# Half of the tail's gate products made inside the sample attention, with a ring of five slots

## The reference

```python
u = rmsnorm(x, g_mix)
proj = jnp.einsum('btd,df->btf', u, w_in)
(q_nsa, kv_nsa, g_nsa, qkv_gdn, b_gdn, a_gdn, z_gdn, q_mem, g_br) = jnp.split(proj, ...)
o_nsa, o_gdn, o_mem = ...            # sparse attention, gated delta rule, attention into memory tokens
gates = jax.nn.sigmoid(g_br.astype(jnp.float32)).reshape(B, T, N_BRANCH, D_MODEL)
merged = (gates[:, :, 0] * jnp.einsum('btc,cd->btd', o_nsa, w_br_nsa)
          + gates[:, :, 1] * jnp.einsum('btc,cd->btd', o_gdn, w_br_gdn)
          + gates[:, :, 2] * jnp.einsum('btc,cd->btd', o_mem, w_br_mem))
h = x + jnp.einsum('btd,de->bte', merged, w_out)
y = h + relu(rmsnorm(h) @ w_ff1)^2 @ w_ff2
```

## Time and profile before

| | |
|---|---|
| median of 3 runs | 1644.3 us (1639.56 to 1644.61) |
| the profiled execution | 1641.88 us, span 1640.1 us |
| mean granted clock | 0.925 |
| PE busy | 1461.0 us (89%) |
| PE weight loads | 1342.2 us (82%) |
| DVE busy | 871.5 us (53%) |
| ACT busy | 383.5 us (23%) |
| DMA | 159 MB, mean 97 GB/s |

### The profile page before, as it was taken

How to read it: one execution, slowest core, us unless ns; L and a number is a source line. 1 busy time by engine, 2 the same in 40 slices (tenths; PEclk the granted TensorE clock), 3 DMA queues, 4 the chain that set the end, 5 groups by cost and what they waited for, 6 DMA issues and landing times. The chain is left out here.

```text
span 1640.1 us, 27038 instructions
## 1 busy us (share of the span) xinstructions
PE 1461.0 (89%) x11343; PEld 1342.2 (82%) x11343; DVE 871.5 (53%) x1590; ACT 383.5 (23%) x891; POOL 82.5 (5%) x76
## 2 busy tenths in 40 slices
PE   6999899889968797989766689999989999999998
PEld 5778789789958586868543389899988999999998
DVE  3555256848633556564433355545746746465563
ACT  3543023222232344454221231000003101000000
POOL 1000001100011111111100000000000000000000
PEclk8999999999967697979678789999999999999999
DMA  9232035151321000010258442333240332323321
GB/s 351 72 116 97 13 95 184 56 201 57 119 53 53 0 1 1 2 52 2 100 190 312 175 124 79 107 99 95 91 156 26 104 104 78 103 80 99 93 88 53
DMA packets 115649, 159.03 MB, mean 97 GB/s; under 512 B 6040, under 2 KB 106840, under 8 KB 112779
## 3 DMA queue, kind: packets, MB, share of 16 engines
q1 hardware_dynamic: 111886, 122.76, 23.4%
q0 software_dynamic: 2304, 33.56, 5.1%
q10 hardware_dynamic: 1348, 1.12, 0.2%
HBM read 145.04 MB, written 16.66 MB: 99 GB/s over the span
## 5 line engine op out<-in xcount | busy, mean ns | idle before, releaser
L330 PE MATMUL ps<-uH,wh 128*128 128x260 f32 x576 | 165.9, 288 | 8.7 <-DVE wt L301 8.7
L330 PE MATMUL ps<-hH,wh 128*128 128x260 f32 x512 | 144.9, 283 | 2.6 <-DVE hT L301 2.6
L330 PE MATMUL ps<-mergedH,wh 128*128 128x260 f32 x512 | 145.7, 285 | 0.0
L330 PE MATMUL ps<-mergedT,wh 128*128 128x260 f32 x512 | 144.8, 283 | 0.0
L330 PE MATMUL ps<-hT,wh 128*128 128x260 f32 x512 | 144.8, 283 | 0.0
L330 PE MATMUL ps<-mergedH,wl 128*128 128x260 f32 x512 | 144.5, 282 | 0.0
L330 PE MATMUL ps<-hH,wl 128*128 128x260 f32 x512 | 144.5, 282 | 0.0
L457 PE MATMUL ps<-XT,w 128*128 128x256 f32 (+1 forms) x512 | 125.5, 386 | 6.3 <-DVE XT L520 6.0
L330 PEld LDWEIGHTS ps<-uH,wh 128*128 128x128 f32 x576 | 109.9, 191 | 13.6 <-DVE wt L301 8.9
L330 PE MATMUL ps<-uL,wh 128*128 128x260 f32 x384 | 109.1, 284 | 0.0
L330 PE MATMUL ps<-uH,tw 128*128 128x260 f32 x384 | 109.0, 284 | 0.0
(11 more groups left out here) (525 smaller groups left out, 3470.8 us busy)
## 6 DMA issues: line engine op xcount, KB each, us to landing
wt<-in_w_ff SPq DMA_DIRECT2D x32, 1024.0 KB, 5.4
wt<-in_w_in SPq DMA_DIRECT2D x15, 1024.0 KB, 5.7
tw<-in_w_in SPq DMA_DIRECT2D x12, 1024.0 KB, 5.3
ring<-in_cache_mem_kv SPq DMA_DIRECT2D x4, 2048.0 KB, 11.2
w<-in_cmp_w SPq DMA_DIRECT2D x8, 512.0 KB, 7.7
ring<-in_cache_win_kv SPq DMA_DIRECT2D x2, 2048.0 KB, 9.8
out_s_win<-in_cache_win_kv SPq DMA_DIRECT2D x1, 4088.0 KB
scratch_uhigh<-uH SPq DMA_DIRECT2D x1, 2080.0 KB
```

The lines of the kernel that those rows point to most:

```text
L330: ins = pe.matmul(out, lhsT(i, c), rhs(j, c), start=(first and c == 0 and k == 0), stop=(last and c == chunks - 1 and k == 2))
```

## The change

1. The gate products of tokens 0 to 255 (`TOKA`) move into the sample attention. A gate tile is made there in two halves of 512 rows, 24 halves in all (`GS`), numbered g. A half is loaded by SP (512 KB, three buffers `gr`), its high part made by ACT (two buffers `gh`), its low part by DVE, and PE makes 24 matmuls of 256 columns into bank 4. After two halves ACT copies the bank to `staged` and SP writes it to memory (256 KB). The steps' places are `gate_keys`.
2. The tail makes gates for tokens 256 to 519 only (264 tokens, two units for each tile in place of four), from the same full weight tiles. It loads the stored sums (`sums`), and ACT takes their sigmoid in one instruction.
3. Weight tiles' high parts are made by ACT in the tail (`highs`); DVE makes the low parts alone.
4. The ring has five slots in place of seven. SP no longer waits for the piece before.
5. `u` of the first 256 tokens is loaded at the stage's start; `u` of the others into the same place after the last half.
6. The scores of the new token are made in the compressed step, kept in `newk`, and read from there.

```diff
-        self.filled = [self.sem(f"e_slot{k}") for k in range(7)]
+        self.filled = [self.sem(f"e_slot{k}") for k in range(5)]
...
+        gate_keys = [0.4, 0.45, 0.7, 5.6, 5.7, 15.5, 19.0, 19.2, 19.4, 25.5, 29.0, 29.2, 29.4, 30.45, 30.7, 35.6, 35.7, 45.5, 49.0, 49.2,
+                     55.5, 55.6, 59.0, 59.2]
+        split_key = lambda g: gate_keys[g - 1] + 0.02 if g else 0.3
...
+            def gate_pe(pe):
+                for g in range(GS):
+                    q, half = g // 2, g % 2
+                    yield gate_keys[g]
+                    pe.wait_ge(g_split, g + 1)
+                    if g == 0:
+                        pe.wait_ge(u_in, 32)
+                    if half == 0 and q:
+                        pe.wait_ge(g_kept, q)
+                    w = g_wh[g % 2], g_low[g % 3]
+                    for m in range(WM):
+                        ins = self.product3(pe, ps[:, 4, TOKA * m:TOKA * (m + 1)], lambda i, c: w[i][:, c, m * P:(m + 1) * P],
+                                            lambda i, c: uA[i][:, HC * half + c, :], HC, first=half == 0 and m == 0, last=half == 1 and m == WM - 1)
+                    ins.then_inc(g_acc, 1)
...
+                def gates():
+                    yield -1.0
+                    for x, dram in zip(uA, self.u_dram):
+                        sp.dma_start(x.bitcast(F32)[:, :, :], dram[:, :, 0:TOKA]).then_inc(u_in, 16)
+                    for g in range(GS):
+                        yield -0.9 if g < 3 else gate_keys[g - 3] + 0.03
+                        if g >= 3:
+                            sp.wait_ge(g_acc, g - 2)
+                        rows = slice(HC * P * (g % 2), HC * P * (g % 2 + 1))
+                        sp.dma_start(g_raw[g % 3][:, :, :], gate_srcs[g // 2][rows, :].rearrange("(c p) n -> p c n", p=P)).then_inc(g_in[g % 3], 16)
+                    yield gate_keys[GS - 1] + 0.03
+                    sp.wait_ge(g_acc, GS)
+                    for x, dram in zip(self.uB, self.u_dram):
+                        sp.dma_start(x.bitcast(F32)[:, :, :], dram[:, :, TOKA:NT]).then_inc(self.u_back, 16)
...
+            def gate_high(act):
+                for g in range(GS):
+                    yield split_key(g)
+                    act.wait_ge(g_in[g % 3], 16 * (g // 3 + 1))
+                    if g >= 2:
+                        act.wait_ge(g_acc, g - 1)
+                    act.copy(g_wh[g % 2][:, :, :], g_raw[g % 3][:, :, :]).then_inc(g_high, 1)
+
+            def gate_sums(act):
+                for q in range(GS // 2):
+                    yield gate_keys[2 * q + 1] + 0.03
+                    act.wait_ge(g_acc, 2 * q + 2)
+                    if q >= 2:
+                        act.wait_ge(g_out[q % 2], 16 * (q // 2))
+                    act.copy(staged[q % 2], ps[:, 4, :].rearrange("p (a n) -> p a n", n=P)).then_inc(g_kept, 1)
...
+            def gate_low(dve):
+                for g in range(GS):
+                    yield split_key(g) + 0.005
+                    dve.wait_ge(g_high, g + 1)
+                    dve.tensor_tensor(g_low[g % 3][:, :, :], g_raw[g % 3][:, :, :], g_wh[g % 2].bitcast(F32)[:, :, :], ALU.subtract).then_inc(g_split, 1)
...
-        return [(m, slice(HALF * h, HALF * h + HALF)) for m in range(WM) for h in range(2)]
+        return [(m, tok) for m in range(WM) for tok in (slice(0, TOKA), slice(TOKA, NT))]
...
+                def sums():
+                    for q in range(Q):
+                        yield start[index["gate", q]] + 0.15 if q >= 2 else 0.05
+                        if q >= 2:
+                            sp.wait_ge(taken, NU * (q - 2) + 3)
+                        sp.dma_start(sig[:, q % 2, :, 0:TOKA], self.gate_dram[q].rearrange("p (m t) -> p m t", m=WM)).then_inc(sums_in[q % 2], 16)
...
+                            yield start[n] + 0.3
+                            act.wait_ge(sums_in[q % 2], 16 * (q // 2 + 1))
+                            act.activation(sig[:, q % 2, :, 0:TOKA], sig[:, q % 2, :, 0:TOKA], ACT.Sigmoid).then_inc(gatedA, 1)
+                            for m in range(WM):
+                                yield unit_at(n, m + 1)
+                                act.wait_ge(acc, acc_of("gate", q, m))
+                                if q >= 2:
+                                    act.wait_ge(taken, NU * (q - 2) + 2 * m + 2)
+                                act.activation(sig[:, q % 2, m, B], ps[:, (WM * q + m) % 2, 0:TOKB], ACT.Sigmoid).then_inc(gated, 1)
+
+                def highs():
+                    for n in range(NT_ + 1):
+                        yield start[n - 1] + 0.18 if n else 0.08
+                        k = k0 + n
+                        act.wait_ge(self.w_loaded[k % 2], self.loaded_at[k])
+                        if n >= 2:
+                            act.wait_ge(acc, self.tile_end[k - 2])
+                        cut = lambda x: x[:, 0:tiles[n][1], :]
+                        act.copy(cut(self.wh[k % 2]), cut(raw[n % 3])).then_inc(self.w_high, 1)
...
-                by_key(dense(), turn(), sample())
+                by_key(highs(), dense(), turn(), sample())
```

More of the change, by code:

```diff
@@ L1849, in stage_sample_attention @@
         ring = self.ring
+        at = self.taken["w1"][1]
+        for name in ("uH", "uL"):
+            self.taken[name] = (at, at + KC * TOKB)
+            at += KC * TOKB
         for k in range(len(ring), RING):
@@ L1969, in cmp_pe @@
                     ins = pe.matmul(rows32(0, j)[:, 0:NCMP], self.qblk[:, 4 * r + j, :], self.kcT[:, 4 * r + j, 0:NCMP], start=True, stop=True)
+                for j in range(4):
+                    for i in range(2):
+                        ins = pe.matmul(rows32(0, j)[:, P + i:P + i + 1], self.qblk[:, 4 * r + j, :], self.knT[:, i, 4 * r + j:4 * r + j + 1], start=True, stop=True)
                 ins.then_inc(c_s[r], 1)
@@ L2094, in load_free, with free_key @@
                         eng.wait_ge(v_done, n + 1)
+            def free_key(k):
+                if k < RING:
+                    return -0.8
+                n = job_of[k - RING]
+                if pieces[k - RING][0] == "memk":
+                    return turn_key(n, GROUPS["mem"] - 1, 3) + 0.05
+                return value_key(n, NPROB(jobs[n][0]) - 1) + 0.05
             @block.gpsimd
@@ L2104, in _ @@
             def _(sp):
[L2105 to L2121, removed]
+                def plain():
+                    for k, (what, r) in enumerate(pieces):
+                        if what == "sel":
+                            continue
+                        yield free_key(k)
+                        load_free(sp, k)
+                        if what == "win":
+                            src = I["cache_win_kv"][4 * r:4 * r + 4].rearrange("b (t p) v g d -> p (b t) (v g d)", p=P)
+                        else:
+                            src = I["cache_mem_kv"][4 * r:4 * r + 4, :, 0 if what == "memk" else 1].rearrange("b (t p) h d -> p (b t) (h d)", p=P)
+                        sp.dma_start(slot(k).rearrange("p (a c) -> p a c", a=src.shape[1]), src).then_inc(fetched[k % RING], 16)
+                    sel_last = max(n for n, (br, _) in enumerate(jobs) if br == "sel")
+                    yield value_key(sel_last, NPROB("sel") - 1) + 0.06
+                    sp.wait_ge(v_done, sel_last + 1)
+                    sp.dma_start(self.tw0[:, :, :], gate_srcs[0].rearrange("(c p) n -> p c n", p=P)).then_inc(self.w_loaded[self.issued % 2], 16)
@@ L2353, in stage_tail @@
         START = 5.0
[L2354 to L2357, removed]
+        start, ends = [START], [0]
+        units_of = lambda n: WM if seq[n][0] == "gate" else NU
+        for n, (kind, _) in enumerate(seq):
+            start.append(start[-1] + units_of(n) * (2.93 if kind == "gate" else 1.44))
+            ends.append(ends[-1] + units_of(n))
+        unit_at = lambda n, i: start[n] + i * (start[n + 1] - start[n]) / units_of(n)
         for n in range(NT_):
-            self.tile_end.append(u0 + NU * (n + 1))
+            self.tile_end.append(u0 + ends[n + 1])
         for n in range(len(tiles)):
@@ L2374, in stage_tail @@
         S = self.local_sem
-        gated, taken, added = (S("m_" + x) for x in ("gated", "taken", "added"))
+        gated, gatedA, taken, added = (S("m_" + x) for x in ("gated", "gatedA", "taken", "added"))
+        sums_in = [S(f"m_sums{i}") for i in range(2)]
+        B = U[1][1]
         turned, oH_kept, oL_kept = (S("t_" + x) for x in ("turned", "oH_kept", "oL_kept"))
@@ L2424, in dense @@
                         w = self.wh[k % 2], low[n % 3]
-                        for i, (m, tok) in enumerate(U):
+                        for i, (m, tok) in enumerate([(m, B) for m in range(WM)] if kind == "gate" else U):
                             yield unit_at(n, i)
-                            u = NU * q + i
+                            u = units_of(n) * q + i
+                            N = tok.stop - tok.start
                             if i == 0:
```

95 lines of the change are left out of this document (56 added, 39 removed).

## The result

The changed kernel takes 1699.0 us (median of 4 runs, 1690.1 to 1701.3), the kernel before 1641.9 us: ratio 1.035, 95% interval 1.032 to 1.038. The forecast was 1659, its range 1620 to 1682. The sign was right, and the size was off by a factor of more than three: +57 us where +17 was forecast.

A forecast was written before the change was run, and what follows sets the result against it. PE was taken to bound the tail, waits the sample attention, where nothing is full. 1641.9 + 74 (attention) - 68 (tail's gain) + 11 (tail's new waits) = 1659 us; range 1620 to 1682.

The forecast's parts named there:

- Start: Attention's start: SP's u and two halves land at about 830, after the gathers; fourth piece done at 844; +18 us.
- Softmax, g5: Job 0's softmax: DVE's low parts of g4 and g5 stand ahead, so it starts 5.5 us late; +5.5 us.
- Values of job 0 to job 1: Attention: memory keys load only now, with five slots, beside two gathers; +14 us, from +11.5 to +17.
- SP first: Job 0's values to job 1's, lower end: memory keys go ahead of the gathers, landing after 9 us; +11.5 us.
- Next four pieces: Job 2 and next selected pieces: g13's and g14's tiles behind gathers hold ACT and DVE before key copies; +9 us.
- The end of the stage: Attention's end: g22 and g23 cost +3.4 us; second load of u covered, up to 5 us if not.
- The clock: Attention: less idle time keeps PE's clock up in transposes and values; -4.5 us.
- Five slots: Attention: 26 us or so of new waiting come with the five slots and the loads.
- The tail: Tail: shorter gate tiles gain 68.0 us, less 11 us for waits on stored sums; about 192 us long.
- The work fills the gaps: Faster rival: loads in time, PE the only bound in the attention; 1615, up to 1630; chance 0.17.
- Slower still: Rival: sums' wait shows in all 10 tail pairs, 22 us, and attention grows by 83; 1679 us; chance 0.16.
- the tail's chain: Tail: ACT's wait for stored sums delays high part, low part and branch product; 2.2 us a pair, 22 at most.

The follow-up runs named there:

- e3: The changed kernel with the splits of halves 5, 9, 13 and 17 put just before their own products: 1684.8 us, attention 234.1.
- e5: The changed kernel with only the first three half tiles loaded, the other 21 loads left out (gates wrong): 1676.9 us, attention 227.0.
- e4: The changed kernel without any gate work in the attention, ring of five slots and 256 KB stores kept: 1621.7 us, attention 173.1.
- e8: The changed kernel with late splits, gathers behind memory keys, second load of u behind stored branch outputs' loads, and late sums' sigmoid: 1678.3 us, ratio 1.022.
- e7: The changed kernel with ACT's sigmoid of the stored sums behind the high part of the next gate tile: 1688.4 us, tail 188.9.
- e11: The kernel before with only the tail's high parts moved to ACT: 1643.3 us against 1640.2, ratio 1.003; tail 253.4.
- e6: The changed kernel with gathers of piece 7 and later held until job 2's memory keys have landed: 1698.3 us, attention 247.6.
- e9: The kernel of e4 with gathers of pieces 7 and up held until job 2's memory keys have landed: 1607.5 us, attention 162.5.

## Why the prediction was wrong

The growth of the attention, phase by phase, from PE's timelines; rows of before are the earlier trace rows:

| phase | before ends | after ends | growth | forecast |
|---|---|---|---|---|
| first four pieces | 823.4 | 843.6 | 20.2 | 18 |
| scores of job 0 | 836.4 | 855.8 | -0.8 | with the clock |
| values of job 0 | 856.4 | 885.5 | 9.7 | 8.3 |
| values of job 1 | 870.4 | 926.7 | 27.2 | 14 |
| next four pieces | 881.4 | 953.7 | 16.0 | 9 |
| values of job 2 | 897.3 | 975.7 | 6.1 | 6.3 |
| values of job 3 | 918.9 | 1002.5 | 5.2 | 7 |
| values of job 4 | 931.9 | 1031.3 | 15.8 | 12.4 |
| end of the stage | 944.7 | 1055.5 | 11.4 | 3.4 |
| sum | | | 110.8 | 78.4, less 4.5 for the clock |

The table's sum is the growth by the tail's start, and holds 0.3 us of a later first matmul. It is 36.9 us above the forecast's 73.9; the largest parts are the values of job 1 (13.2), the end of the stage (8.0), the next four pieces (7.0) and the clock (4.5 less 0.8). The tail gave 3 us less than forecast, and the rest of the miss lies in the stages around.

- **Start: the time right, the order in part.** g0 waited for its split until 831.0 (about 830 was forecast), and the fourth piece was through at 843.6 (844). But not all of SP's loads came after the gathers. `uH`, issued 0.7 us ahead of the first gather, landed after 7.5 us, and only `uL` and the tiles behind it took 18 us and more.
- **Softmax, g5: right.** The mechanism (DVE's low parts ahead of the softmax) shows as the 3.6 us at 867.3, and the late splits (e3) took it away.
- **Values of job 0 to job 1: the step that failed.** It costed the memory keys' landing (16.5 us if the gathers go first) and nothing behind them. They landed after 18, and then g9's tile had still to land, with the copies of the keys behind it. The forecast named this mechanism for g13 and missed it for g9, which stands behind both memory pieces in the same key order. e5 and e3 show it: without the load, or with the split put later, the wait of 6.5 us is gone and the phase is 8.0 us shorter in both, 33.2 us in place of 41.2. That is the larger part of the 13.2 us by which the phase was off. The 33.2 us are still 2 above the forecast's upper end of 31, for the later landing (18 and not 16.5 us) and slower turning of the keys and scores (9.5 and not 8 us). And it took 14 between its own ends of 11.5 and 17; the end "SP first" could not come. In the changed kernel and in e4 the gathers passed SP's keys although these were issued 0.2 us ahead.
- **Next four pieces: mechanism right, term mis-sized.** 16.0 in place of 9 (7 to 11). g13 waited for its split as forecast (5.5 us), and then ran at the lower clock, 5.1 us for the half instead of 2.8. The other 5 us of this phase are not taken apart.
- **The end of the stage: the cover named was not there.** The second load of u was costed at nothing, with 5 us if uncovered. SP issued it ahead of the small loads that DVE's last steps need. DVE waited 7.8 us for them where it had waited 0.2:

```profile
939.42 2.10 DVE L2283 TENSOR_TENSOR ring<-ring,gate 8x512 f32<-8x512 f32 x3 [0.20 <-DMA ring<-scratch_win]
...
1050.14 2.10 DVE L2376 TENSOR_TENSOR ring<-ring,gate 8x512 f32<-8x512 f32 x3 [7.77 <-DMA ring<-scratch_win]
```

  With the load put behind them (e8) DVE waits 0.9 us and PE's idle time is 5.8 us less, of the 8.0 us by which this phase was off.
- **The clock.** The forecast took 4.5 us off because less idle time keeps the clock up. Only the 0.8 us in the scores of job 0 show as a gain; the stage's mean rose from 0.77 to 0.81, but g0, g7, g13 and g21, each behind a wait, took 4.5 to 5.3 us in place of 2.8.
- **Five slots.** The prediction put 26 us of new waiting on the slots and the loads together; e4 measured 36.5 without the gate work's loads.
- **The tail: the sum right, the parts not quite.** 53.9 us less against 57. Of the 14 us that the gain of 68.0 lost, some 6 were the sums' wait (e7; it is 5.9 us from a gate tile's issue at 1155.7 to ACT's release at 1161.6, 6.3 was forecast), and 3 to 5 the longer chain of the high parts, if they weigh there as in the kernel before (e11); that is not shown for the changed tail. The prediction gave that part nothing of its own. Its pair of 13.8 us without sample work came out at 13.6.
- **The range.** Its upper end, 1682, lay 3 us above the sum of the phases' upper ends and the tail's whole chain (1679). It had no room for a term that was missing, and in a stage with so many waits in order such a term was to be expected.
- **The rivals.** "The work fills the gaps" failed where it was said to be decided: at the memory keys and the window piece. "Slower still" was right in its sign, but by the attention (110.5 us more, where it had 83), not by the tail's chain, which was mostly covered.

## What to carry to other kernels

Filling idle time of an engine pays only if the filler's inputs have their own place in every queue: list, for each moved step, the transfers ahead of its tile and the instructions behind the one that waits for it, on all engines. A buffer that is given up to make room for it is a cost of its own, to be measured alone first; here five slots alone were a third of the attention's growth and more than half of the 54 us that the tail gave. Where a step waits for a load, put its conversion just ahead of its use, not just behind the last user of its buffer.

## What the runs showed of the hardware

A load of 2 MB by SP that was issued just ahead of two gathers of 2 MB (0.2 us in e4) landed 18 to 19 us after its issue beside them, and 9 to 10 us after it with the gathers held back (e6, e9). Two stores of 64 KB by ACT beside two gathers took 9.4 and 11.4 us in the changed kernel, where the earlier trace rows has 8.9 and 9.1: SP's loads of 6 MB were then beside them too. SP's loads do not stand still altogether: `uH` (1 MB, issued 0.7 us ahead of the first gather) landed after 7.5 us, and the gathers took 13.3 us in place of 10.6. `uL`, issued in the same moment as the first gather, took 18.1 us. From 805 to 850 us the profile counts 288 packets for the gathers' 4.19 MB and 7840 for 7.60 MB of SP's. The Trainium skill, DMA: Bandwidth & Descriptors, section "Queues, rings and completion order", says that a DMA engine takes turns between its queues but changes only after a whole packet of descriptors; the order of landing in these runs fits that and not an even share of the bytes. That this rule is the cause is argued and not shown, and how many descriptors a packet has, no run here shows.

The granted clock: a half of 24 matmuls took 2.8 to 3.1 us in a busy stretch, 5.3 us after 12.1 us of idle time (g0) and 5.1 us after 5.5 us (g13 at 944.3). After 2.0 us it took 4.5 us once (g7 at 890.6) and 3.0 us once (g19 at 1007.6). So an uncovered wait cost its length and, in the half behind it, between nothing and 2.5 us more.
